# Decode attention: the value pages are fetched from ScalarE's queue, the key pages stay on SyncE's

## What is computed

```python
def gather(pool):                      # cache_k, cache_v: (pages, 128, 16 heads, 64)
    g = pool[page_table]               # page_table: (8 sequences, 32 pages)
    return g.reshape((db, n_pages * pool.shape[1]) + pool.shape[2:])

def fox_attend(q, k, v, cq, ck, q_pos, k_pos):
    s = jnp.einsum('bqhd,bkhd->bhqk', q, k) * (HEAD_DIM ** -0.5)
    s = s + (cq[..., :, None] - ck[..., None, :])
    s = jnp.where(k_pos[None, :] <= q_pos[:, None], s, min)
    p = jax.nn.softmax(s, axis=-1)
    return jnp.einsum('bhqk,bkhd->bqhd', p, v)
```

## Time and profile before

| | |
|---|---|
| median of 3 runs | 2609.51 us |
| the profiled execution: its time, its span | 2603.24 us, 2601.6 us |
| busy share of the span: TensorE, VectorE, ScalarE, GpSimd | 91%, 53%, 37%, 36% |
| mean granted TensorE clock | 0.954 of full speed |
| moved by DMA in all / by SyncE's queue | 426.90 MB / 362.03 MB |
| page transfers of keys and of values, both from SyncE | 256 and 256, 512 KB each |
| attention stage: share of the DMA engines' time, rate | mostly 0.9 to 1.0, 340 to 400 GB/s |

### The profile page before, as it was taken

The page is one execution under the profiler, slowest core; times in us unless marked ns, Lnnn a source line. Parts: engine busy times, 40 slices in busy tenths (PEclk is TensorE's granted clock), DMA queues, the critical chain, the costliest instruction groups (busy, mean ns, idle before and its releaser), DMA issues.

```text
span 2601.6 us, 45870 instructions
## 1 busy us (share of the span) xinstructions
PE 2356.9 (91%) x15044; PEld 1853.8 (71%) x15044; DVE 1377.9 (53%) x1904; ACT 970.7 (37%) x1679; POOL 926.3 (36%) x526
## 2 busy tenths in 40 slices
PE   5999999996459989799888997999998999899899
PEld 4999999995259989689888995444444444344399
DVE  4788998888880022355534671344443444434423
ACT  4556665654440022233113232433433334233311
POOL 0799888898572124212332232010010000000121
PEclk7999999998669999899999998999999999999999
DMA  2222222221133121112231246999998998989312
GB/s 107 71 71 70 75 71 79 71 71 56 34 113 113 42 67 41 57 50 83 86 106 61 74 124 265 397 387 356 332 403 286 357 364 324 360 319 355 137 51 79
DMA packets 131250, 426.90 MB, mean 164 GB/s; under 512 B 23601, under 2 KB 32434, under 8 KB 130162
## 3 DMA queue, kind: packets, MB, share of 16 engines
q1 hardware_dynamic: 112594, 362.03, 38.2%
q0 software_dynamic: 15872, 51.34, 5.6%
q10 hardware_dynamic: 2592, 11.14, 1.1%
HBM read 387.19 MB, written 39.35 MB: 164 GB/s over the span
## 4 chain that ended last, share of the span: by engine, by line
PE 63%; POOL 12%; DVE 9%; issue 8%; ACT 5%; DMA 2%; ACTq 0%; SPq 0%; POOLq 0%; DVEq 0%
PE PS L471 10%; PE PS L473 10%; PE PS L472 9%; POOL ACC L1185 7%; PE PS L665 6%; PE PS L703 5%; PE PS L731 5%; PE PS L752 5%; PE PS L686 3%; PE PS L769 3%; POOL WL L1158 2%; PE PS L479 2%; PE PS L660 2%; POOL ACC L1181 1%; PE PS L740 1%
## 5 line engine op out<-in xcount | busy, mean ns | idle before, releaser
L1456 DVE SCALAR_TENSOR_TENSOR PS<-UX,CWT,PS 128x1024 f32<-128x1024 f32 (+1 forms) x672 | 466.2, 781 | 0.0
L1158 POOL TENSOR_TENSOR WL<-RAW,WH 128x1024 fp32r<-128x1024 f32 (+1 forms) x113 | 295.8, 2618 | 367.4 <-ACT WH L817 358.9
L504 PE MATMUL PS<-HH,WH 128*128 128x384 f32 (+1 forms) x1152 | 379.3, 329 | 20.7 <-DVE HL L1442 20.7
L506 PE MATMUL PS<-HH,WL 128*128 128x384 f32 (+1 forms) x1152 | 378.2, 328 | 0.0
L505 PE MATMUL PS<-HL,WH 128*128 128x384 f32 (+1 forms) x1152 | 378.1, 328 | 0.0
L471 PE MATMUL PS<-GH,WH 128*128 128x384 f32 (+1 forms) x792 | 268.3, 339 | 48.6 <-DVE GL L1529 28.9
L1185 POOL TENSOR_TENSOR ACC<-ACC,PROD 128x1088 f32<-128x1088 f32 x112 | 284.7, 2542 | 31.3 <-ACT PROD L869 25.1
L473 PE MATMUL PS<-GH,WL 128*128 128x384 f32 (+1 forms) x792 | 264.8, 334 | 0.0
L472 PE MATMUL PS<-GL,WH 128*128 128x384 f32 (+1 forms) x792 | 263.5, 333 | 0.0
L504 PEld LDWEIGHTS PS<-HH,WH 128*128 128x128 f32 x1152 | 217.8, 189 | 24.7 <-issue 13.7
L1653 DVE TENSOR_REDUCE MXP<-PS 128x1 f32<-128x1024 f32 (+7 forms) x128 | 96.8, 756 | 235.4 <-PE PS L665 235.3
(11 more groups left out here) (225 smaller groups left out, 4277.3 us busy)
## 6 DMA issues: line engine op xcount, KB each, us to landing
KV<-ck SPq DMA_DIRECT2D x256, 512.0 KB, 8.1
KV<-cv SPq DMA_DIRECT2D x256, 512.0 KB, 6.1
RAW<-wA SPq DMA_DIRECT2D x48, 512.0 KB, 3.5
RAW<-wB SPq DMA_DIRECT2D x33, 512.0 KB, 3.5
RAW<-wP SPq DMA_DIRECT2D x16, 640.0 KB, 4.0
zT_scr<-ZS ACTq DMA_DIRECT2D x16, 544.0 KB, 2.7
Z<-zT_scr SPq DMA_DIRECT2D x16, 544.0 KB, 3.6
RAW<-wO SPq DMA_DIRECT2D x16, 512.0 KB, 3.6
```

The costliest lines, as they stand in the source:

```text
L504: pe.matmul(out, WH[w][:, kk], HH[:, k, a:b], start=k == 0, stop=False)
L506: mm = pe.matmul(out, WL[w][:, kk], HH[:, k, a:b], start=False, stop=k == KD - 1)
L1158: pool.tensor_tensor(WL[s][:, 0:n], RAW[s][:, 0:n], WH[s][:, 0:n].bitcast(F32), ALU.subtract).then_inc(s_lo, 1)
L1456: i = dve.scalar_tensor_tensor(out=o, in0=x, scalar=w[:, j:j + 1], in1=o, op0=ALU.mult, op1=ALU.add)
```

## The change

SyncE's `pages(b)` now covers the eight key groups only. A new helper `value_pages(b, t)` of ScalarE loads the four page numbers of value group t and issues the four transfers, with the same wait on `s_dd` as before. ScalarE calls it at the end of steps 4, 5, 6 and 7 for groups 8, 9, 10 and 11, and at the end of steps 10, 11, 12 and 13 for groups 12, 13, 14 and 15. The tiles, the transfers and what the consumers wait for are the same.

```diff
@@ SyncE
             def pages(b):
-                for t in range(16):
+                for t in range(NG):
                     for kk in range(GP):
-                        page = sp.value_load(PTAB[0:1, ds(NPG * b + GP * (t % NG) + kk, 1)], min_val=0,
+                        page = sp.value_load(PTAB[0:1, ds(NPG * b + GP * t + kk, 1)], min_val=0,
                                              max_val=ck.shape[0] - 1)
                         if kk == 0 and (started(b) or t >= 4):
                             sp.wait_ge(s_dd, 16 * b + t - 3)
-                        sp.dma_start(KV[t % 4][:, kk, :], at(ck if t < NG else cv, page)).then_inc(s_kv[t % 4], 16)
+                        sp.dma_start(KV[t % 4][:, kk, :], at(ck, page)).then_inc(s_kv[t % 4], 16)
@@ ScalarE, att_step
                         act.activation(SC[:, 512 * t:512 * t + 512], PS[:, 4, :], ACT.Copy).then_inc(s_sc, 1)
+                        if t >= 4:
+                            value_pages(b, t + 4)
                         continue
...
                     if j == 0:
                         decode_keys_first(b, t)
+                    if 2 <= j < 6:
+                        value_pages(b, t + 2)
+
+            def value_pages(b, t):
+
+                for kk in range(GP):
+                    page = act.value_load(PTAB[0:1, ds(NPG * b + GP * (t - NG) + kk, 1)], min_val=0,
+                                          max_val=cv.shape[0] - 1)
+                    if kk == 0:
+                        act.wait_ge(s_dd, 16 * b + t - 3)
+                    act.dma_start(KV[t % 4][:, kk, :], at(cv, page)).then_inc(s_kv[t % 4], 16)
```

## The result

The changed kernel takes 2679.05 us (median of 4 runs, 2678.77 to 2692.06), the kernel before, beside it, 2608.24 us. The ratio is 1.0285, with a 95% interval of 1.0253 to 1.0317: slower by 2.9%. (A ratio here is estimated over all runs of both kernels, and is not the quotient of the two medians.) The profiled execution has a span of 2677.4 us, 75.8 us more than before.

What follows compares the result with a forecast made beforehand. The prediction took TensorE to set the time, with the DMA engines close behind. Its sum was 2603.2 + 41 (ScalarE's hold-up) + 17 (later transfers) = 2661 us, range 2604 to 2715 us.

Steps and rivals of the forecast that it cites:

- Both signs: Register work running beside activations more than allowed, or late transfers costing several microseconds at each change of b.
- The cost of a group: Four page loads and issues on ScalarE, taken at SyncE's cadence: 1.09 us a page, 4.36 us a group.
- Step 8: Group 11's issue on ScalarE delays the copy PT, for which the output product waits: 1.5 us lost.
- Step 12: Group 13's issue, behind the decode exponential, delays ScalarE's copy PTD and the decode product: 1.8 us lost.
- Step 14: Group 15's issue delays PTD, 1.0 to 1.3 us lost; group 14's pages land about in time.
- Step 15: Group 15's pages land 0 to 4 us late beside the next key pages; 2.5 us taken, in seven iterations.
- The two terms: ScalarE's hold-up, 7 x 4.6 + 8.5 = 41 us, and the later transfers, 17 us with range 0 to 28.
- The clock: Each stall drops TensorE's clock as at the loop's jump: up to 30 us more, once an iteration.
- b = 0: First iteration, steps shorter without an output product, so ScalarE overhangs more: 8.5 us lost.
- Rival (a): The issues fit in ScalarE's idle time, at most 2.6 us a group; no change, 2603 us, chance 0.12.
- Rival (b): Fewer pages in flight shorten TensorE's pause at the loop's jump: at most 15.6 us, 2588 us, chance 0.09.
- rival (c): Loads wait for ScalarE's activation, 2684 us, or stalls drop the clock; both 2714 us; chance of dearer 0.18.

Runs made afterwards that it cites:

- e8: Kernel before, all pages on SyncE, with ScalarE doing the same loads and issues at the same places for small 128-row transfers into an unused tile; 2636.90 us, ratio 1.0117.
- e7: Kernel before, all pages on SyncE, with the fourth key group of each iteration started one step later; 2604.15 us, ratio 0.9987.

## Why the prediction was right, and where it was not

The measured 2679 us lies in the range and in the forecast's own case (2630 to 2685), 18 us above the 2661 of the sum. The two causes that it named are the two that the runs show, but their sizes are not, and that the sum came near owes something to luck. Both signs under which it called itself wrong came true: register work ran beside activations more than it allowed (step 12 below), and late transfers cost 6.0 us at each of the seven changes of b (41.8 / 7). Point by point:

- **What bounds the kernel**: right. SyncE's queue had nothing to give, and no run that moved value pages off it became faster.
- **The cost of a group**: 4.36 us forecast, 4.42 measured. On ScalarE the load takes 281 ns and the issue 349 (min/median/max ns):

```profile
L1130 ACTq TENSOR_LOAD <-PTAB x256: 274/281/489, 1629.5 to 2497.0; - x128
...
L1134 ACTq DMA_DIRECT2D KV<-cv x248: 344/349/986, 1640.4 to 2497.7; - x124
```

  The Trainium skill's floor of about 600 ns for a `tensor_load` ("DMA: Bandwidth & Descriptors", "Latency and other measured facts") does not hold on this engine either; the measurement decides.
- **Step 8**: 1.5 us forecast, 1.54 measured where the clock did not drop (b = 4 and 6; 1.25 in b = 0, which has no output product). With a half-clock stretch behind it the same overrun costs 2.9 to 4.6 us. The mechanism was right and the term was short of the clock.
- **Step 12**: 1.8 us forecast, 0.4 to 1.0 measured. The failed step is the start of the block, which I put behind the last exponential. In b = 3 of the changed kernel, ScalarE and then TensorE:

```profile
2011.01 0.91 ACT L1099 ACTIVATE PP<-PS,NMX 128x768 f32<-128x768 f32 x1
2011.62 0.35 ACTq L1134 DMA_DIRECT2D KV<-cv  x1
...
2011.88 0.73 ACT L1145 ACTIVATE SC<-SC,NGM 128x512 f32<-128x512 f32 x1
...
2012.75 2.89 ACTq L1134 DMA_DIRECT2D KV<-cv  x3
2015.82 0.60 ACT L1140 ACTIVATE PTD<-PS 128x512 f32<-128x512 f32 x1 [3.11 <-issue]
...
2016.51 0.41 PE L686 MATMUL PS<-FCON,PP 128*128 128x128 f32 x2 [0.81 <-issue]
```

  The first issue stands while `PP` still runs and ahead of the decode exponential's start, although it comes after both in the program. ScalarE's queue runs ahead of its arithmetic, so one of four pages was hidden there. Nor did line 752 get the waits for ScalarE that I forecast (5.2 us in six waits, as before). The late `PTD` (its end is 2016.42) meets TensorE a little earlier: the prompt transposes of line 686 that go to bank 6 have to wait until `PTD` has emptied it. I also read ScalarE's own work in such a step too short, 2.7 us where the earlier trace rows give 0.60 + 2.45 = 3.05; no term hung on it.
- **Step 14**: wrong in its reason. I had 1.0 to 1.3 us of a late `PTD`, and group 14's pages landing just in time. Measured are 1.5 to 3.8 us, all of a late landing: e8, with the same blocks, shows nothing in step 14, and neither does b = 7. Group 15's block began early in the same way: in b = 3 its first issue stands at 2024.95, while `PP` (2024.33 to 2025.01) still runs. For the landing I let the DMA engines work at 404 GB/s from the first issue, 10.4 us for group 14 and one key group; they moved 311 GB/s from 2018 to 2025, group 15 and a second key group came in from 2025 on, and group 14's last page landed 14.1 us after the first was issued.
- **Step 15**: 2.5 us forecast from 0 to 4, measured 2.8 to 4.3 in the seven iterations. I took the middle where the upper end was right, and again without the clock.
- **The two terms**: ScalarE's was 41 us and measured 29 (22.7 + 6.6), that of the late transfers was 17 and measured 42 (18.3 + 23.5). The errors partly cancel; the sum is better than its parts. An undisturbed b grew to 113.2 us, not 110.5.
- **The clock**: I had it as a rival's price of up to 30 us, outside the sum. TensorE's busy time grew by 29.7 us. It should have been a term: the stall that I forecast for step 8 brought a half-clock stretch in five of eight iterations.
- **b = 0**: 8.5 us forecast for ScalarE alone; steps 8 and 12 together grew by 2.3. The longer overhang without an output product did not come. The growth of this iteration is 13.7 in all, of which 7.7 are steps 14 and 15 and 3.7 steps 2 and 3.
- **Rival (a)** needed 2.6 us a group and falls with 4.42. The Trainium skill's sentence that the issue time saved is "usually small relative to the DMA itself" ("DMA: Bandwidth & Descriptors", "Issuing engines are not separate DMA queues") is no guide here: 4.42 us of ScalarE stand against about 5.2 us for moving a group. The same page, under "Queues, rings and completion order", has each DMA engine take turns between the queues that have work. The trace agrees: with both queues full, each got half of the bytes (1.27 and 1.23 MB), and the landing of groups 14 and 15 rose from 5.2 to 8.4 and 11.6 us; serving pages in the order of their issue would look much the same, as the two queues' issues alternate. **Rival (b)** stays open: e7 had about as many pages queued when the pause began as the kernel before, and the changed kernel, which had fewer, paused once for less and once for more. Of **rival (c)**, the dearer load falls, the clock holds.

## What to carry to other kernels

The cost of issuing from a compute engine is not the sum of its idle time against the sum of the issues; it is the length of the block against the shortest gap between two things that others wait for. Moving the same 256 issues by a step or two and splitting one block took the loss from 71 us to 3.8, inside the measurement's 0.2%. Where the DMA engines are at 95%, a stretch in which they are left idle can come back as somebody's late page. It did in the changed kernel and with all pages on SyncE two steps late, and it did not with the issues one step earlier. Holding back one of two queues moved the lateness to the other.

## What the runs showed that I had not expected

- A wait of TensorE of about 2 us sometimes lowered the granted clock and sometimes did not, at the same place of different iterations. In step 8 the growth is 1.54 us without a drop (b = 4, 6) and 4.5 to 4.6 us with a long stretch at half clock, the 1.2 GHz level (b = 3, 5). The stretch of b = 3, then the same place in b = 4 at full clock (the last three columns are the clock, and the DMA engines' share and rate):

```profile
1983.90:1990.70 6.80, 5.67 (x31) 3.54 (x31) 2.10 (x7) 2.88 (x11) 1.84 (x4) 0.50 0.93 243
2105.50:2112.30 6.80, 4.49 (x43) 3.09 (x42) 2.75 (x9) 3.52 (x12) 4.01 (x7) 1.00 1.03 308
```

  Fewer matmuls (31 against 43) take more busy time.
- The issue of a DMA is not one price: 0.35 us for 128 rows into SBUF, whether rows of 4096 or of 8 bytes, but 0.51 us for a copy of 16 x 64 bytes from HBM to HBM.
- ScalarE's queue issues a DMA while one activation ahead of it is unfinished and the next has not begun (the rows under step 12).
